# Moving key rotation, key zeros, sums of squares and an exponential table out of the first attention heads of a two-layer diffusion step

## Chip, cores and metric

One core of a Trainium2 chip (trn2) runs the whole program once. The metric is the device time of one execution in microseconds. Times below are device times or places in one profiled execution, counted from the start of its span.

## What is computed

The reference is one inference step of a two-layer backbone over 640 tokens (512 latent tokens of an 8 x 64 grid, 128 context tokens) with a model width of 1024. Each layer does:

```python
h = modulate(xs, norm_mix_g[l], sh_a, sc_a)            # RMSNorm, shift, scale
q_mla, c_kv, k_rope, na_q, na_k, na_v, gq, gk, gv = mixer_inputs(h, w_in[l], ...)
# MLA: c_q, c_kv are RMS-normed columns of z = h @ w_in; q_mla = c_q @ w_q_up; k_rope is rotated
# GQA: gq (6 heads) and gk (2 heads) are RMS-normed per head of 64, scaled, then rotated
o_na  = neighbourhood_attention(na_q, na_k, na_v, cache_na_k, cache_na_v, na_rpb)  # 4 heads
o_mla = blocked_attention(q_mla, [k_lat, k_ctx], [v_lat, v_ctx])                   # 6 heads
o_gqa = blocked_attention(rope(gq), [rope(gk), cache_gqa_k], [gv, cache_gqa_v])    # 6 heads
xs = xs + g_a * mix_out(o_mla, o_na, o_gqa, w_out[l])
xs = xs + g_f * swiglu(modulate(xs, ...), w_gate[l], w_up[l], w_down[l])
```

Context tokens attend only to context tokens. After the second layer comes one last RMSNorm. Keys and values of the context tokens are outputs too.

## The kernel before

Everything is fp32. A product with weights is three matmuls (`split_mm`, L631 to L633): both operands are split into a high part that ScalarE (ACT) rounds off and a low part that VectorE (DVE) gets by subtracting it (`lo`, L1323). So nearly every tile that TensorE (PE) reads has passed through ACT first and DVE second.

A layer has three stages. **Projection:** `z = h @ w_in` in 6 chunks of 304 columns, each chunk 5 tiles of 128 tokens. Tile number n = 5 * chunk + token tile goes to bank n % 6 of PSUM, ACT copies it to `z` (L1177), and PE starts tile n only when tile n - 6 has been copied. At the end of chunk 3 ACT sums squares of the MLA columns (L1192, L1194). In layer 0 DVE also has dot products for the modulation (`ada`, L1338), two per tile, some of them in each chunk. **Attention:** 16 heads, first 4 NA heads, then 6 MLA and 6 GQA heads. A head is 5 units: 4 blocks of 128 latent queries (i = 0 to 3) and the context block (i = 4). **Output projection and FFN.**

The order of work in the attention stage is one list, `SCHED`, made by `schedule()`. All engines walk through this same list, each doing its own part of every step. The list is cut in slots, one for each unit u = 5 * head + i: step `S` comes first in a slot, then what `extra` puts into it. Each engine executes strictly in order, so a step that waits holds up all that stands behind it on its engine. The steps that matter here:

- `S`: PE computes the scores (L846, L848 for NA heads), DVE adds the bias (L1562) and takes the maximum (L1568), ACT does the exponential of the unit before (L1132), DVE and POOL the reciprocal and the scaling (L495, L514) of the unit before that. PE needs the exponential of unit u - 2 for its bank.
- `M`: preparation of the next head's keys and queries: PE transposes (L702), ACT copies (L1081, L1069, L1078), DVE makes the low parts; `C`: cached keys (L1055, L1421, L1323). Steps `M` share bank 7, so each waits for the DVE part of the one before.
- `T`: transposition of the probabilities (L873, L1223, L1323), followed by the product with V.
- `CL`: DVE's low parts of the latents, two of 512 columns of `cqT` (L1460) and one of `ckvT`. `QU` n = 0 to 9: PE's product of `cqT` with `w_q_up` for one half of a token tile (6 matmuls of 288 columns), followed on ACT by the copy to `qm` (L1112). `CT`: the latents of the context tile, needed by QU 8 and 9. `QR` and `KR`: rotation of `qm` and of the MLA key by POOL (GpSimd; L1701, L1704, L1706). `BM`: POOL makes the bias of a head (L1765). `WK`: split of `w_kv_up`.
- `GS`, `GR` (layer 0 only): squares (ACT L1159) and sums (DVE L1485) of the GQA columns, one step for each token tile in slots 8 to 19, and the square root (L1163) in slot 21. In layer 1 the same squares and sums are done in the projection stage instead, at the end of chunk 3 on ACT and after the last split on DVE. `GZ`: scaling and rotation of the GQA columns (in layer 1 mostly before the heads).

The low parts of the keys have 64 rows of zeros for NA and GQA heads, set by DVE (L1421) when a head with new keys begins. `keep_busy` (L665) issues matmuls whose result is not used.

Of the kernel before, what the change touches and what calls it, by code (L numbers as in the profile page):

```python
# [19 lines left out]
F32 = mybir.dt.float32  # L20
# [5 lines left out]
P = 128  # L26
# [17 lines left out]
IC = 6  # L44
# [60 lines left out]
def schedule():  # L105
# [101 lines left out]
def build(nc, a, out):  # L207
    ctx = ExitStack()
    with ctx:
# [20 lines left out]
        warm = sb("warm", [P, 1])  # L230
# [142 lines left out]
        still_set = sem("still_set")  # L373
        win_first = sem("win_first")
# [254 lines left out]
        def _(pe):  # L629
# [132 lines left out]
            for l in range(DEPTH):  # L762
# [55 lines left out]
                for s in SCHED:  # L818
                    if s[0] == "S":
# [31 lines left out]
                        if u < 2:  # L851
                            keep_busy(4, 3)
                        if u == 9:
                            pe.wait_ge(qm_done, l * 2 * NT + 2 * NT)
                        if kind == "na" and u >= 9:
                            keep_busy(1, 2)
                    elif s[0] == "T":
# [19 lines left out]
                        def pv(g=g, mt=mt, n=n, a0=a0, a1=a1):  # L877
                            pair, slot = g // 2, g % 2
                            if slot == 0 and mt == 0:
# [133 lines left out]
        def _(sc):  # L1013
# [124 lines left out]
            for l in range(DEPTH):  # L1138
# [34 lines left out]
                for c in range(IC):  # L1173
                    for t in range(NT):
# [3 lines left out]
                        if c == 4 and t == (NT - 1 if (l == 0) else 1):  # L1178
# [9 lines left out]
                    if c == 3:  # L1188
# [20 lines left out]
                for s in SCHED:  # L1209
# [24 lines left out]
                    elif s[0] == "QU":  # L1234
# [11 lines left out]
                    elif s[0] == "GS" and l == 0:  # L1246
                        g_square(s[1], ztmp[:])
                    elif s[0] == "GR" and l == 0:
                        g_rms()
# [11 lines left out]
                sc.activation(warm[:], eps[:], ACT.Sqrt)  # L1261
                for o in range(KD):
# [6 lines left out]
                    if o == 2 and l + 1 < DEPTH:  # L1269
                        sc.wait_ge(cond_in, 32)  # L1270
                        sc.activation(silu_f[:], silu_f[:], ACT.Silu).then_inc(silu_done, 1)
                        sc.activation(warm[:], eps[:], ACT.Sqrt)
# [13 lines left out]
                sc.activation(warm[:], eps[:], ACT.Silu)  # L1286
# [23 lines left out]
                sc.activation(warm[:], eps[:], ACT.Sqrt)  # L1310
# [562 lines left out]
```

## Time and profile before

| | us |
|---|---|
| median of 3 runs | 1838.56 (1837.71 to 1839.36) |
| the profiled execution, own time | 1841.04 |
| its span in the profile | 1839.2 |
| PE busy | 1711.2 (93%) |
| DVE busy | 1164.6 (63%) |
| ACT busy | 692.7 (38%) |
| POOL busy | 215.3 (12%) |
| mean granted TensorE clock | 0.972 of full speed |

The profile follows one execution of the program. Its busy shares are averages over stages with different limits, so a stage has to be looked at by itself. Line numbers (L1568) are lines of the kernel; a tile is named without its buffer number. A number in brackets behind a row is the idle time of that engine just before the instruction, with the instruction that ended it.

### The profile page before, as it was taken

The numbers are of one execution on the slowest core, as the hardware profiler recorded it, in microseconds if no ns is written. First come the engines' busy times: TensorE is split into PE (matmuls) and PEld (weight loads), VectorE is DVE, ScalarE is ACT, GpSimd is POOL, SyncE is SP. The second block draws the span as 40 slices with busy tenths as digits, with TensorE's granted clock in tenths as the row PEclk, the third lists the DMA queues.
The fourth block names the chain that finished last, engine by engine and source line by source line (L and its number), as shares of the span: only waits on it lengthen the run. The fifth ranks groups of instructions, "written<-read, shape, count | busy, mean of one in ns | idle before, by whom it ended". The sixth has DMA issues, their size and how long they took to land.

```text
span 1839.2 us, 28458 instructions
## 1 busy us (share of the span) xinstructions
PE 1711.2 (93%) x11360; PEld 1657.6 (90%) x11360; DVE 1164.6 (63%) x2215; ACT 692.7 (38%) x1359; POOL 215.3 (12%) x316
## 2 busy tenths in 40 slices
PE   6899879889899999999989988988989999999997
PEld 6898777779899999999989977877989999999997
DVE  5996868848777777667552576786354544444443
ACT  2434756842422222222143376676342222222221
POOL 0003543310000000000010272332000000000001
PEclk9999999999899999999989989999989999999997
DMA  9461000053444433333132010002212222222201
GB/s 351 160 220 60 9 1 3 1 171 104 141 157 145 152 114 125 126 125 126 50 89 82 10 43 0 2 1 90 72 47 91 69 94 88 69 68 68 69 23 57
DMA packets 105525, 159.78 MB, mean 87 GB/s; under 512 B 5024, under 2 KB 83680, under 8 KB 105184
## 3 DMA queue, kind: packets, MB, share of 16 engines
q1 hardware_dynamic: 102800, 153.26, 24.8%
q10 hardware_dynamic: 2160, 3.23, 0.5%
q0 software_dynamic: 480, 2.19, 0.4%
q8 instruction: 49, 0.80, 0.2%
q14 instruction: 36, 0.29, 0.1%
HBM read 155.09 MB, written 3.57 MB: 86 GB/s over the span
## 4 chain that ended last, share of the span: by engine, by line
PE 82%; DVE 9%; ACT 3%; issue 2%; DMA 2%; POOL 1%; SPq 0%; POOLq 0%; DVEq 0%; ACTq 0%
PE ps L631 25%; PE ps L633 24%; PE ps L632 24%; PE ps L873 2%; PE ps L639 2%; DVE ps L1338 1%; DVE negmax L1568 1%; PE ps L846 1%; PE ps L848 1%; DMA ada_n<-in_w_ada_first 1%; DVE hT L1323 1%; DMA wo_raw<-in_w_out 1%; PE ps L702 1%; POOL rstd L1721 1%; DVE K L1323 1%
## 5 line engine op out<-in xcount | busy, mean ns | idle before, releaser
L631 PE MATMUL ps<-hT,gw 128*128 128x320 f32 x1408 | 437.6, 311 | 6.8 <-DVE hT L1323 6.8
L632 PE MATMUL ps<-hT,gw 128*128 128x320 f32 x1408 | 437.2, 311 | 0.0
L633 PE MATMUL ps<-hT,gw 128*128 128x320 f32 x1408 | 437.2, 310 | 0.0
L1402 DVE SCALAR_TENSOR_TENSOR x<-ps,mod,x 128x320 f32<-128x320 f32 (+2 forms) x576 | 211.6, 433 | 97.3 <-PE ps L633 94.3
L631 PEld LDWEIGHTS ps<-hT,gw 128*128 128x128 f32 x1408 | 265.8, 189 | 7.3 <-issue 7.3
L632 PEld LDWEIGHTS ps<-hT,gw 128*128 128x128 f32 x1408 | 265.8, 189 | 0.0
L633 PEld LDWEIGHTS ps<-hT,gw 128*128 128x128 f32 x1408 | 265.6, 189 | 0.0
L1654 DVE TENSOR_TENSOR mm<-sl,ps 128x320 f32<-128x320 f32 x88 | 42.7, 488 | 320.3 <-issue 185.3
L631 PE MATMUL ps<-act,dw 128*128 128x320 f32 x704 | 218.0, 310 | 2.7 <-DVE act L1323 2.7
L633 PE MATMUL ps<-act,dw 128*128 128x320 f32 x704 | 217.9, 309 | 0.0
L632 PE MATMUL ps<-act,dw 128*128 128x320 f32 x704 | 217.9, 309 | 0.0
L1293 ACT ACTIVATE sl<-ps 128x320 f32<-128x320 f32 x88 | 38.3, 438 | 445.6 <-PE ps L633 445.6
L631 PE MATMUL ps<-wi,hT 128*128 128x304 f32 x480 | 146.9, 306 | 12.1 <-DVE hT L1323 12.1
L633 PE MATMUL ps<-wi,hT 128*128 128x304 f32 x480 | 146.4, 305 | 0.0
L632 PE MATMUL ps<-wi,hT 128*128 128x304 f32 x480 | 145.8, 304 | 0.0
L631 PEld LDWEIGHTS ps<-act,dw 128*128 128x128 f32 x704 | 132.2, 188 | 2.9 <-DVE act L1323 2.9
L1300 ACT ACTIVATE act<-mm 128x320 fp32r<-128x320 f32 x88 | 41.3, 472 | 243.2 <-DVE mm L1654 243.2
L632 PEld LDWEIGHTS ps<-act,dw 128*128 128x128 f32 x704 | 132.2, 188 | 0.0
L633 PEld LDWEIGHTS ps<-act,dw 128*128 128x128 f32 x704 | 132.2, 188 | 0.0
L1718 POOL TENSOR_TENSOR rstd<-sq 128x640 f32<-128x640 f32 x2 | 3.1, 1566 | 1096.7 <-ACT sq L1022 1096.7
L1323 DVE TENSOR_TENSOR pT<-ps,pT 128x512 fp32r<-128x512 f32 (+2 forms) x176 | 109.1, 622 | 23.9 <-ACT pT L1223 22.4
L514 POOL TENSOR_SCALAR probs<-probs,rinv 128x640 f32<-128x640 f32 (+2 forms) x128 | 98.2, 768 | 180.5 <-DVE rinv L495 180.2
(212 smaller groups left out, 3574.7 us busy)
## 6 DMA issues: line engine op xcount, KB each, us to landing
ada_w<-in_w_adaT SPq DMA_DIRECT2D x48, 512.0 KB, 5.9
gw_raw<-in_w_gate SPq DMA_DIRECT2D x22, 1024.0 KB, 5.4
gw_raw<-in_w_up SPq DMA_DIRECT2D x22, 1024.0 KB, 8.0
dw_raw<-in_w_down SPq DMA_DIRECT2D x22, 1024.0 KB, 4.9
ada_wf<-in_w_adaT SPq DMA_DIRECT2D x34, 512.0 KB, 6.7
wi_raw<-in_w_in SPq DMA_DIRECT2D x12, 1216.0 KB, 6.7
wo_raw<-in_w_out SPq DMA_DIRECT2D x16, 512.0 KB, 5.1
ada_wq<-in_w_adaT SPq DMA_DIRECT2D x10, 512.0 KB, 4.8
```

The source lines that it names most:

```text
L514: po.tensor_scalar(t, t, rinv[:, u:u + 1], 1.0, ALU.mult, ALU.mult).then_inc(p_ready, 1)
L631: pe.matmul(dst, lh, rh, start=start, stop=False, skip_group_check=True)
L632: pe.matmul(dst, lh, rl, start=False, stop=False, skip_group_check=True)
L633: return pe.matmul(dst, ll, rh, start=False, stop=stop, skip_group_check=True)
L639: m = pe.matmul(ps[:, bank, 2 * t:2 * t + 2], tile[:, t * P:(t + 1) * P], ones[:, 0:2], start=first and t == 0, stop=last, skip_group_chec ...
L702: m = pe.transpose(ps[0:64, bank, o0:o0 + P], z[:, t, c0:c0 + 64], ident[:])
L873: m = pe.transpose(ps[:, 4 + n % 2, i * P:(i + 1) * P], probs[:, g % 2, i, pos:pos + P], ident[:])
L1293: sc.activation(sl[:, hf_], ps[:, 4 * j + hf_, 0:HALF], ACT.Silu).then_inc(sl_ready, 1)
L1300: sc.activation(act[:, j, 0, hf_ * HALF:(hf_ + 1) * HALF], mm[:, hf_], ACT.Copy).then_inc(act_hi, 1)
L1323: return ve.tensor_tensor(dst, src, f(hi), ALU.subtract)
L1402: i = ve.scalar_tensor_tensor(out=x[:, o, c0:c1], in0=ps[:, banks + hf_, s0:s0 + c1 - c0], scalar=mod[:, l, part * KD + o, q:q + 1], in1=x ...
L1654: ve.tensor_tensor(mm[:, hf_], sl[:, hf_], ps[:, 4 * j + 2 + hf_, 0:HALF], ALU.mult).then_inc(mm_ready, 1)
```

## The change

In `schedule()` the steps of the first slots are placed by hand. `CL` moves from slots 0 and 1 to slots 1 and 2. `QU` moves from the second half of slots 2 to 5 to slots 3 to 6, from slot 4 on ahead of the other extras; its copy on ACT becomes a step of its own (`QE`) at the slot's end. `CT` moves from slot 6 to the head of slot 7, `QU` 8 and 9 to the heads of slots 8 and 9. `KR`, `GS` and `GR` leave the list. PE's product waits for two `CL` steps and no longer for three; the first product with V waits for the third. DVE no longer clears key rows for NA heads, and does so only for GQA heads; POOL clears the low parts of all keys at once after the last split of `w_in`, and rotates the MLA keys after chunk 1. Layer 0 does squares, sums and root of the GQA columns where layer 1 does. After the root ACT executes one exponential on one column in both layers. `keep_busy(4, 3)` follows the first three units, before the first two.

```diff
-    spread([("CL", 0), ("CL", 1), ("CL", 2)], 0, 2)
-    for n in range(8):
-        extra[2 * (2 + n // 2) + 1].append(("QU", n))
-    extra[13].append(("CT", 3))
-    extra[15].append(("QU", 8))
-    extra[17].append(("QU", 9))
-    spread([("KR", t) for t in range(4)], 1, 4)
+    extra[3] += [("CL", 0), ("CL", 1)]
+    extra[5] += [("CL", 2)]
+    for n in range(0, 8, 2):
+        extra[6 + n] = [("QU", n), ("QU", n + 1)] + extra[6 + n]
+        extra[7 + n] += [("QE", n), ("QE", n + 1)]
+    extra[14] = [("CT", 3)] + extra[14]
+    for n in range(8, 10):
+        extra[2 * n] = [("QU", n)] + extra[2 * n]
+        extra[2 * n + 1].append(("QE", n))
     spread([("QR", t) for t in range(4)], 5, 8)
-    spread([("GS", t) for t in range(NT)] + [("GR",)], 8, 16)
...
-                pe.wait_ge(cT_ready, l * 4 + (3 if t < 4 else 4))
+                pe.wait_ge(cT_ready, l * 4 + (2 if t < 4 else 4))
...
-                        if u < 2:
+                        if u < 3:
                             keep_busy(4, 3)
-                        if u == 9:
+                        if u == 10:
                             pe.wait_ge(qm_done, l * 2 * NT + 2 * NT)
-                        if kind == "na" and u >= 9:
+                        if kind == "na" and u >= 10:
...
+                            if n == 0:
+                                pe.wait_ge(cT_ready, l * 4 + 3)
                             pe.wait_ge(pT_ready, l * TS + n + 1)
...
-                            if not (l == 0):
-                                g_rms()
+                            g_rms()
+                            sc.activation(warm[:, 3:4], eps[:], ACT.Exp)
...
-                        if l:
-                            sc.wait_ge(z_done, l * IC * NT + G_CHUNKS * NT)
-                            for t in range(NT):
-                                g_square(t, rstd[:, 0:512])
+                        sc.wait_ge(z_done, l * IC * NT + G_CHUNKS * NT)
+                        for t in range(NT):
+                            g_square(t, rstd[:, 0:512])
...
-                    elif s[0] == "QU":
+                    elif s[0] == "QE":
                         queries_out(l, s[1])
...
-                if kind == "gqa" or kind == "na" and h < 2:
+                if kind == "na" and h == 0:
+                    ve.wait_ge(key_zeros, l + 1)
+                if kind == "gqa":

                     ve.memset(K[64:P, kb, 1, :].bitcast(F32), 0.0)
...
-                        if l:
-                            for t in range(NT):
-                                g_sum(t, rstd[:, 0:512])
-                            g_mean()
+                        for t in range(NT):
+                            g_sum(t, rstd[:, 0:512])
+                        g_mean()
                     if l == 0:
                         for t in REST[REST_AT[c]:REST_AT[c + 1]]:
                             ada(l, t)
...
+                po.wait_ge(z_done, l * IC * NT + 2 * NT)
+                for t in range(4):
+                    if t:
+                        po.wait_ge(q_roped, l * 8 + t)
+                    rotate(l * OWN + 3 * t, 1, 32, z[:, t, OFF_KR:OFF_G].unsqueeze(1), rope[:, t, 0, 64:96], rope[:, t, 1, 64:96],
+                           rstd[:, LAT:LAT + 32].unsqueeze(1)).then_inc(q_roped, 1)
+                po.wait_ge(wi_ready, l * IC + IC)
+                settled(po, passed_po)
+                po.memset(K[:, :, 1, :].bitcast(F32), 0.0).then_inc(key_zeros, 1)
                 po.wait_ge(dots, 2 * dot_at(l, NADA - 1 if l else REST[-1]) + 2)
                 po.memset(still[:].bitcast(F32), 0.0).then_inc(still_set, 1)
```

## Rows read from the trace of the kernel before

**Rows 1.** The page: the chain that ended last, by engine.

```profile
PE 82%; DVE 9%; ACT 3%; issue 2%; DMA 2%; POOL 1%; SPq 0%; POOLq 0%; DVEq 0%; ACTq 0%
```

**Rows 2.** Both attention stages: stretch, length, busy us of PE, PEld, DVE, ACT, POOL, clock, DMA.

```profile
160.45:390.00 229.55, 196.83 (x1261) 171.26 (x1261) 178.19 (x403) 159.91 (x400) 97.84 (x149) 0.97 0.05 14
1058.75:1278.00 219.25, 194.92 (x1261) 171.41 (x1261) 169.57 (x386) 153.81 (x390) 86.81 (x138) 0.97 0.05 15
```

**Rows 3.** Timeline, DVE maxima: units 19, 21, 23 of layer 0, then 10, 19, 21, 23 of layer 1.

```profile
221.15 0.27 DVE L1568 TENSOR_REDUCE negmax<-ps 128x1 f32<-128x128 f32 x1
226.40 0.81 DVE L1568 TENSOR_REDUCE negmax<-ps 128x1 f32<-128x640 f32 x1
233.83 0.81 DVE L1568 TENSOR_REDUCE negmax<-ps 128x1 f32<-128x640 f32 x1
...
1093.33 0.56 DVE L1568 TENSOR_REDUCE negmax<-ps 128x1 f32<-128x384 f32 x1
1117.66 0.27 DVE L1568 TENSOR_REDUCE negmax<-ps 128x1 f32<-128x128 f32 x1
1124.96 0.82 DVE L1568 TENSOR_REDUCE negmax<-ps 128x1 f32<-128x640 f32 x1
1130.28 0.80 DVE L1568 TENSOR_REDUCE negmax<-ps 128x1 f32<-128x640 f32 x1
```

**Rows 4.** Stretch from unit 0 to unit 10 of layer 0.

```profile
165.69:195.32 29.63, 24.47 (x145) 22.21 (x144) 22.67 (x55) 20.71 (x59) 24.12 (x50) 0.83 0.13 38
```

**Rows 5.** Timeline, first slots of layer 0: PE's and DVE's waits around the products.

```profile
172.17 0.61 PE L631 MATMUL ps<-wq,cqT 128*128 128x288 f32 x1
...
175.22 0.41 PE L846 MATMUL ps<-K,Q 128*128 128x256 f32 x1
...
178.63 0.35 PE L631 MATMUL ps<-wq,cqT 128*128 128x288 f32 x1
...
180.28 0.28 PE L846 MATMUL ps<-K,Q 128*128 128x256 f32 x1
...
176.20 0.43 DVE L1562 TENSOR_TENSOR ps<-ps,bias_h 128x256 f32<-128x256 f32 x1 [2.21 <-PE ps L848]
...
180.89 0.43 DVE L1562 TENSOR_TENSOR ps<-ps,bias_h 128x256 f32<-128x256 f32 x1 [1.70 <-PE ps L848]
```

**Rows 6.** Timeline, ACT: table load of the first exponential; PE: what it releases.

```profile
167.47 1.28 ACT L1132 ACT_TABLE_LOAD   x1
...
169.49 0.45 PE L846 MATMUL ps<-K,Q 128*128 128x384 f32 x1 [0.58 <-ACT probs L1132]
```

**Rows 7.** Timeline, DVE: the zeros of head 1.

```profile
166.47 0.70 DVE L1421 MEMSET K<- 64x768 f32 x1 [0.22 <-issue]
```

**Rows 8.** Stretches at half clock, one in each layer.

```profile
171.00:177.60 6.60, 6.04 (x25) 5.61 (x26) 3.97 (x11) 3.68 (x13) 5.17 (x12) 0.50 0.16 48
1120.00:1123.40 3.40, 3.40 (x15) 3.30 (x16) 1.49 (x5) 0.80 (x2) 0.51 (x1) 0.51 0.00 0
```

**Rows 9.** Timeline, end of layer 0's projection: DVE, ACT; last, a sum in layer 1.

```profile
139.62 1.22 DVE L1338 SCALAR_TENSOR_TENSOR ps<-ada_wq,silu_c 128x1024 f32<-128x1024 f32 x1
...
150.25 0.21 DVE L1533 RECIPROCAL stat<-stat 128x10 f32<-128x10 f32 x1
...
160.98 0.70 DVE L1421 MEMSET K<- 64x768 f32 x1 [7.17 <-ACT K L1055]
...
146.64 0.42 ACT L1177 ACTIVATE z<-ps 128x304 f32<-128x304 f32 x1 [2.82 <-PE ps L633]
...
1034.27 0.69 DVE L1485 TENSOR_REDUCE stat<-rstd 128x8 f32<-128x512 f32 x1 [0.70 <-ACT rstd L1159]
```

**Rows 10.** DVE beside POOL: one scaling in layer 1; a POOL key rotation; chunks 2 to 5.

```profile
1048.48 1.78 DVE L1497 TENSOR_TENSOR z<-z,stat 128x512 f32<-128x512 f32 x1
...
176.49 0.25 POOL L1706 TENSOR_TENSOR z<-z,rstd 128x32 f32<-128x32 f32 x1
...
93.60:139.60 46.00, 46.00 (x332) 46.00 (x332) 44.38 (x62) 17.21 (x38) 0.00 (x0) 1.00 0.68 226
```

More of the change, by code:

```diff
@@ L229, in build @@
         eps = sb("eps", [P, 1])
-        warm = sb("warm", [P, 1])
+        warm = sb("warm", [P, 4])
         b_ada = sb("b_ada", [P, DEPTH, NADA])
@@ L373, in build @@
         still_set = sem("still_set")
+        key_zeros = sem("key_zeros")
         win_first = sem("win_first")
@@ L1177, in _ @@
                         sc.activation(z[:, t, c * ICW:(c + 1) * ICW], ps[:, n % 6, 0:ICW], ACT.Copy).then_inc(z_done, 1)
-                        if c == 4 and t == (NT - 1 if (l == 0) else 1):
+                        if c == 4 and t == (NT - 1 if l == 0 else 1):
                             sc.wait_ge(cstat_ms, 2 * l + 1)
                             sc.activation(stat[:, :, 0:2], stat[:, :, 0:2], ACT.Sqrt).then_inc(cstat_rms, 1)
-                            if not (l == 0):
-                                g_rms()
+                            g_rms()
+                            sc.activation(warm[:, 3:4], eps[:], ACT.Exp)
                     if c + 2 < IC:
@@ L1245, in _ @@
                         sc.activation(ckvT[:, 0, LAT:640], kc_mla[:], ACT.Copy).then_inc(wqk_hi, 1)
[L1246 to L1249, printed above, removed]
                     elif s[0] == "V":
@@ L1259, in _ @@
                         i.then_inc(v_hi, 1)
-                sc.activation(warm[:], eps[:], ACT.Sqrt)
+                sc.activation(warm[:, 0:1], eps[:], ACT.Sqrt)
                 for o in range(KD):
@@ L1271, in _ @@
                         sc.activation(silu_f[:], silu_f[:], ACT.Silu).then_inc(silu_done, 1)
-                        sc.activation(warm[:], eps[:], ACT.Sqrt)
+                        sc.activation(warm[:, 0:1], eps[:], ACT.Sqrt)
                 def gw_split(b, j):
@@ L1285, in _ @@
                 modulated(l, 1)
-                sc.activation(warm[:], eps[:], ACT.Silu)
+                sc.activation(warm[:, 0:1], eps[:], ACT.Silu)
                 def ffn_block(b, last):
@@ L1309, in _ @@
                 ffn_block(FB - 1, True)
-                sc.activation(warm[:], eps[:], ACT.Sqrt)
+                sc.activation(warm[:, 0:1], eps[:], ACT.Sqrt)
                 sc.wait_ge(act_ready, (l + 1) * FB * 4 + 1)
@@ L1594, in _ @@
                         lo(ckvT[:, 1, LAT:640], kc_mla[:], ckvT[:, 0, LAT:640]).then_inc(wkv_ready, 1)
-                    elif s[0] == "GS" and l == 0:
-                        g_sum(s[1], ztmp[:])
-                    elif s[0] == "GR" and l == 0:
-                        g_mean()
                     elif s[0] == "V":
@@ L1729, in g_rotate @@
                         po.wait_ge(g_roped, l * 4 + t)
-                    rotate(l * OWN + (24 if l == 0 or t >= LATE_G else 0) + 3 * t, 8, 64, view, rope[:, t, 0, 0:64], rope[:, t, 1, 0:64], tmp).then_inc(g_roped, 1)
+                    rotate(l * OWN + (24 if l == 0 or t >= LATE_G else 12) + 3 * t, 8, 64, view, rope[:, t, 0, 0:64], rope[:, t, 1, 0:64], tmp).then_inc(g_roped, 1)
                     po.wait_ge(g_roped, l * 4 + t + 1)
@@ L1746, in _ @@
                 value_zeros(0)
-                turned = 0
                 for s in SCHED:
@@ L1770, in _ @@
                             window(po, l, h + 1)
-                    elif s[0] in ("KR", "QR"):
+                    elif s[0] == "QR":
                         t = s[1]
-                        if s[0] == "QR":
-                            po.wait_ge(qm_done, l * 2 * NT + 2 * t + 2)
-                        if turned:
-                            po.wait_ge(q_roped, l * 8 + turned)
-                        if s[0] == "KR":
-                            n, view = 1, z[:, t, OFF_KR:OFF_G].unsqueeze(1)
-                        else:
-                            n, view = 6, qm[:, t, :].rearrange("p (h d) -> p h d", h=6)[:, :, 64:96]
-                        tmp = rstd[:, 0:32 * n].rearrange("p (h d) -> p h d", h=n)
-                        rotate(l * OWN + (3 * LATE_G if l else 0) + 3 * turned, n, 32, view, rope[:, t, 0, 64:96], rope[:, t, 1, 64:96],
+                        po.wait_ge(qm_done, l * 2 * NT + 2 * t + 2)
+                        po.wait_ge(q_roped, l * 8 + 4 + t)
+                        view = qm[:, t, :].rearrange("p (h d) -> p h d", h=6)[:, :, 64:96]
+                        tmp = rstd[:, 0:192].rearrange("p (h d) -> p h d", h=6)
+                        rotate(l * OWN + 12 + (3 * LATE_G if l else 0) + 3 * t, 6, 32, view, rope[:, t, 0, 64:96], rope[:, t, 1, 64:96],
                                tmp).then_inc(q_roped, 1)
-                        turned += 1
                     elif s[0] == "S":
```

## The prediction, made before the changed kernel was run

> **What bounds the kernel now.** I read the chain of waits first: 82% of it is PE, 9% DVE [rows 1], so a change away from PE pays only where PE waits. Then the busy time by stretch. The attention stages are the loose places: layer 0 spends 229.6 us there with PE busy 196.8, layer 1 219.3 us with PE busy 194.9, for the same matmuls [rows 2]. The two layers run one schedule, so I put the maxima of DVE side by side, unit by unit, which is the view that prices this change. From unit 10 (195.32, where the stretch of rows 4 ends) to unit 19, layer 0 takes 25.83 us and layer 1 24.33 [rows 3, 4]: the squares and sums cost 1.50 us there. From unit 21 to 23 layer 0 takes 7.43 and layer 1 5.32 [rows 3]: 2.11 us for the square root, which switches ACT's table away from the exponential and back. The first 10 units take 29.63 us, of which DVE is busy 22.67 [rows 4], so 7 us of its time are waits. The large ones are for PE: 2.21 and 1.70 us [rows 5], each for scores queued behind two query products. That queueing is what the new order addresses. The end of an attention stage releases the next weights and PE's output projection, so I pass each microsecond saved there on to the end.
>
> **Squares, sums, root (layer 0).** Removed from the heads: 1.50 + 2.11 = 3.6 us. One of the five squares lies before unit 10, and I take 0.2 for it, since DVE was waiting there anyway: 3.8 us, between 3.4 and 4.1.
>
> **Their new place.** ACT does square 0 at once, but for square 1 it waits for DVE's first sum, and that stands behind the last weight split, which ends just before the dots at 139.62 [rows 9]. Behind ACT's wait stand its copies of `z`. In layer 1 one round of square and sum takes 0.69 + 0.70 = 1.39 us [rows 9]. So the sums end about 4 x 1.39 + 0.7 = 6.3 us later, at 145.9, the last square at about 145.1, and the first held copy (tile 20) at 145.5. PE needs it for tile 26, which it starts when tile 25 ends, at 146.64 [rows 9]: 1.1 us of slack. DVE's dots, 139.62 to 150.25, end at 156.5, and what follows them is late by the same 6.3 us; before, DVE then stood idle for 7.17 us until 160.98 [rows 9]. It fits, narrowly. The root adds nothing there, as ACT is waiting for PE. The sum has 0.3 us of loss for this item, the range 0 to 2.9 (below).
>
> **POOL's new work before the heads.** Four key rotations of four short instructions, 0.25 us or less each [rows 10], after chunk 1, and one clearing of the keys after the last split. Nothing else is queued on POOL: its next item waits for the dots. But DVE is busy 44.38 of the 46.00 us of that stretch [rows 10], so what it loses there moves the first sum. One DVE instruction of layer 1 took 1.78 us beside POOL [rows 10], where the sum of equal size took 0.69. If each of 16 rotations delays DVE by its own 0.25, that is 4.0 us, less 1.1 slack = 2.9; if none does, 0. I take about 1.4, since the short ones mostly fall into gaps between dots: 0.3 after the slack. The Trainium skill ("SBUF — State Buffer", "SBUF: two separate sides") has the rule that speaks against this part: a DVE instruction with two SBUF inputs and a GpSimd instruction that reads SBUF exclude each other for a whole instruction. By it the loss would be at the 2.9 end.
>
> **The exponential's table.** The first exponential waits for 1.28 us of table load in each layer, and PE's third unit stood 0.58 us for it [rows 6]. Early, the load meets an idle ACT. Alone it is worth 0.6 (PE's wait) to 1.28 us a layer; it is inside the next sum. The Trainium skill ("ScalarE: Activation LUTs", "What ACT_TABLE_LOAD costs") gives 2.66 us for a switch, with a drain of 1.38. By it the heads would gain up to 1.4 more a layer. The trace shows 1.28 alone: the root's two loads cost 2.11 together.
>
> **Zeros and key rotation.** Head 0's clearing lay under ACT's key copies: worth 0. Head 1's 0.70 us [rows 7] counts only as DVE work removed. POOL's scaling was not what PE waited for, so the rotation's place is worth 0 by itself; what covers it is POOL's lead of some microseconds in slots 5 to 8.
>
> **The query products.** In the new list the scores of unit 3 go before products 0 and 1, so DVE's 2.21 us wait goes, and the scores of unit 5 stand behind products 2 and 3 alone, which go out while DVE splits V: the 1.70 us goes too. With the 0.70 of clearing that is 4.6 us a layer. What is late next: products 4 and 5 now stand ahead of the key transposes of head 2 in PE's queue, two products that take 1.65 us at full clock (178.63 to 180.28) and 3.05 at half (172.17 to 175.22) [rows 5]. ACT's copies and DVE's low part of head 2's keys start that much later against unit 5, and products 6 and 7 wait for ACT, whose `qm` copies stand behind those key copies. A pair of products at full clock is 1.65 us, a little of it covered by DVE's own work, so I take back 1.3: **3.3 us a layer.** Ends: 4.6 if later slack swallows it, 1.3 if only the table counts. The extra `keep_busy` (3 matmuls) stands where PE waits for the exponential and the next queries: 0.
>
> **Sum.** 2 x 3.3 + 3.8 - 0.3 = 10.1 us. The profiled execution's 1841.04 gives 1830.9; the median of the runs is 2.5 us lower, so against it I predict **1828.5**. 0.2%, some 3.7 us, is about what a measurement of this kernel can tell from no change.
>
> **Rivals.**
> *The clock goes with the waits (20%).* Products 0 to 3 ran at a granted clock of 0.50 [rows 8], the lower of its levels (1.2 GHz), after PE had idled three times while it waited for head 1's low parts and the exponential. If PE still idles enough before them, or in the new wait for ACT's copies, 4 of the 8 products run at half: 1.4 us for each pair. Then, or if the table is not kept to the first exponential (1.3 a layer), the heads give 1.5 a layer: 3.0 + 3.8 - 0.3 = 6.5, 1832.0. For: both layers show this stretch. Against: PE has three more matmuls and scores ahead of the first product.
> *The first heads give it back (8%).* If DVE or POOL is the bound of units 5 to 15, whatever PE gains is waited away, and only layer 0's 3.5 remains: 1835.1, no change that can be told. For: DVE is busy 22.67 and POOL 24.12 of 29.63 us [rows 4]. Against: differences between the layers stay from one unit to the next once they arise, and POOL loses four rotations of about 1.1 us there.
> *More than that (8%).* The clock fell in layer 1 at 1120 and not in layer 0: units 19 to 21 took 7.30 against 5.25 [rows 3, 8]. Without it, and with 4.6 a layer, the gain is 9.2 + 3.8 + 2.05 = 15: 1823.5.
> *Slower (2%).* Place: ACT's queue in layer 0's projection, where one late sum holds all copies of `z` and through them PE's tile 26. It decides once the first sum is late by 1.1 + 10.1 us. Behind the dots (10.6 us), delayed by POOL (4.0), and each sum lengthened as in rows 10 (5 x 1.1 = 5.5), that is 20.1 - 1.1 = 19.0 us of stall, less 10.4: 1847. Against: in the code the sums stand ahead of the dots.
>
> **How the numbers follow.** The forecast has 62%, with a range of its own from 1825.5 (4.6 a layer) to 1832 (2.9 lost, 2.8 a layer). The first rival lies at its upper end; to take in the clock's share at both ends and part of the larger gain the range is 1824.0 to 1833.5, leaving out the 8% near 1835, the slower case and about half of the larger one. Faster by over 0.2% (below 1834.9): 62 + 20 + 8 = 90%; same 8%; slower 2%.
>
> **What would show it.** Right: unit 10 of each layer 2.8 to 4 us nearer to unit 0; layer 0 like layer 1 from unit 10 to 23 but for clock stretches; a table load at L1183 or so beside an idle ACT; no root among the heads; attention stages of about 222 and 216 us. A step is wrong if PE shows idleness before tile 26 (squares' place), if DVE's dots grow beyond 1.23 us after chunk 1 (POOL), if a pair of products takes 3 us (clock), or if DVE waits over 1.3 us for head 2's keys (order). The forecast is wrong if layer 0's projection grows by more than 3 us, or if unit 20 lies no earlier than before.

## Result, and the profile after

| | before | after |
|---|---|---|
| median of 6 runs each, same chip, us | 1838.25 (1835.68 to 1839.36) | **1828.37** (1825.34 to 1832.24) |
| ratio to before, 95% interval | | 0.995 (0.9939 to 0.996) |
| the profiled execution, own time / span | 1841.04 / 1839.2 | 1825.34 / 1823.5 |
| its mean granted clock | 0.972 | 0.981 |

The gain of the medians is 9.9 us; 10.1 were predicted. The two profiled executions differ by 15.7, because the one of before is among its slowest and the one of after is the fastest of its six. So the traces say where time went, and the medians how much. Of the 15.7 us, 11.9 lie between the first and the last unit of the two layers' heads and 0.3 ahead of them. The other 3.5 lie in the stages between and behind the heads, where half-clock stretches fell differently.

The page after: the busy line, the granted clock in 40 slices and the chain that ended last, by engine.

```profile
PE 1697.8 (93%) x11362; PEld 1644.9 (90%) x11362; DVE 1162.3 (64%) x2211; ACT 689.9 (38%) x1359; POOL 233.1 (13%) x318
PEclk9999999999999999999979999999989999999998
PE 77%; DVE 13%; ACT 4%; issue 3%; DMA 2%; POOL 1%; SPq 0%; POOLq 0%; DVEq 0%; ACTq 0%
```

POOL is busy 18 us longer although it has two instructions more; why is below. Stretches of after, columns as in [rows 2]: both attention stages, the first ten units of both layers [rows 4], and chunks 2 to 5 of the projection [rows 10].

```profile
160.45:383.00 222.55, 192.44 (x1262) 167.45 (x1262) 173.87 (x395) 152.89 (x390) 94.44 (x133) 0.99 0.05 14
1050.00:1264.30 214.30, 190.02 (x1262) 166.47 (x1262) 168.20 (x384) 152.06 (x389) 82.36 (x122) 1.00 0.05 15
165.38:191.75 26.37, 20.91 (x146) 18.59 (x144) 21.83 (x53) 18.63 (x58) 20.08 (x31) 1.00 0.14 43
1055.39:1081.15 25.76, 20.52 (x143) 18.28 (x142) 22.04 (x53) 18.71 (x57) 19.11 (x31) 1.00 0.14 43
93.60:139.60 46.00, 46.00 (x333) 46.00 (x332) 44.38 (x60) 16.31 (x35) 16.07 (x16) 1.00 0.68 226
```

The attention stages lost 7.0 and 5.0 us. The ten units lost 3.26 in layer 0 and 3.67 in layer 1, and their clock is full where it was 0.83 in layer 0. DVE's maxima of units 10, 19, 21 and 23 of layer 0 [rows 3]:

```profile
191.75 0.56 DVE L1568 TENSOR_REDUCE negmax<-ps 128x1 f32<-128x384 f32 x1
...
216.11 0.27 DVE L1568 TENSOR_REDUCE negmax<-ps 128x1 f32<-128x128 f32 x1
...
221.96 0.81 DVE L1568 TENSOR_REDUCE negmax<-ps 128x1 f32<-128x640 f32 x1
...
227.14 0.81 DVE L1568 TENSOR_REDUCE negmax<-ps 128x1 f32<-128x640 f32 x1
```

Unit 10 to 19 takes 24.36 us (25.83 before), 19 to 21 5.85 (5.25), 21 to 23 5.18 (7.43): 3.1 us in all. For the experiments I measure each unit's maximum from that of unit 0. Unit 14 is there because the first ten units turned out not to hold the whole effect. Each * stands for 3.4 us at half clock before that mark. That is 1.7 us of full-speed time, but the mark moves by less where PE has waits that take it up.

| us after unit 0 | L0: 6 | 10 | 14 | 19 | L1: 6 | 10 | 14 | 19 |
|---|---|---|---|---|---|---|---|---|
| before | 18.35** | 29.63*** | 41.08*** | 55.46*** | 18.17** | 29.43*** | 39.96*** | 53.76*** |
| before_busy3 | 16.36 | 26.97 | 38.56 | 52.94 | 16.32 | 26.83 | 38.45 | 52.24 |
| order_only | 16.63 | 28.75* | 40.25* | 54.64* | 16.58 | 27.29 | 38.45 | 52.23 |
| old_order | 16.20 | 27.35* | 37.89* | 51.68* | 16.12 | 26.26 | 36.79 | 50.58 |
| kr_back | 16.28 | 26.58 | 38.66 | 52.46 | 16.25 | 28.32* | 38.90* | 52.69* |
| wait3 | 18.56* | 28.59* | 39.16* | 52.96* | 18.72* | 28.74* | 39.32* | 53.11* |
| after | 16.36 | 26.37 | 36.95 | 50.73 | 16.01 | 25.76 | 36.34 | 50.12 |
| after_again | 16.29 | 26.30 | 36.89 | 50.68 | 16.24 | 26.04 | 36.63 | 50.42 |
| keys_first | 14.84 | 24.81 | 35.39 | 49.17 | 14.88 | 26.85* | 37.38* | 51.18* |

The first slots of layer 0 after, timeline, as in [rows 5, 6]: PE's waits at the query products, then DVE's, then ACT's first exponential.

```profile
171.58 0.40 PE L633 MATMUL ps<-wq,cqT 128*128 128x288 f32 x1 [0.56 <-DVE cqT L1461]
...
174.98 0.37 PE L633 MATMUL ps<-wq,cqT 128*128 128x288 f32 x1 [0.96 <-ACT qm L1116]
...
181.09 0.37 PE L633 MATMUL ps<-wq,cqT 128*128 128x288 f32 x1 [1.28 <-ACT qm L1116]
...
177.25 0.43 DVE L1562 TENSOR_TENSOR ps<-ps,bias_h 128x256 f32<-128x256 f32 x1 [0.25 <-PE ps L850]
...
180.54 0.68 DVE L1322 TENSOR_TENSOR K<-ps,K 64x512 fp32r<-64x512 f32 x1 [2.02 <-ACT K L1085]
...
167.31 0.58 ACT L1136 ACTIVATE probs<-ps,negmax 128x384 f32<-128x384 f32 x1
```

The waits of 2.21 and 1.70 us are gone, and the exponential starts without a load. DVE now waits 2.02 us for head 2's keys, and PE 1.28 for ACT's copies of products 4 and 5.

### The profile page after: what moved, and what is told of

Its sections match the earlier page's. It is cut to its first block, busy times and chain, and to the rows that moved or that the text cites. A ratio compares the mean times of both kernels' runs of the same rounds, so it can differ in the third digit from the quotient of the medians.

```text
span 1823.5 us, 28464 instructions
## 1 busy us (share of the span) xinstructions
PE 1697.8 (93%) x11362; PEld 1644.9 (90%) x11362; DVE 1162.3 (64%) x2211; ACT 689.9 (38%) x1359; POOL 233.1 (13%) x318
## 4 chain that ended last, share of the span: by engine, by line
PE 77%; DVE 13%; ACT 4%; issue 3%; DMA 2%; POOL 1%; SPq 0%; POOLq 0%; DVEq 0%; ACTq 0%
PE ps L633 23%; PE ps L635 22%; PE ps L634 22%; DVE ps L1337 5%; PE ps L875 2%; PE ps L641 2%; DVE negmax L1568 1%; PE ps L848 1%; DVE hT L1322 1%; PE ps L704 1%; DMA ada_n<-in_w_ada_first 1%; PE ps L850 1%; DMA wo_raw<-in_w_out 1%; DVE K L1322 1%; POOL rstd L1717 1%
```

## Experiments

The kernels ran in three jobs. Before's median was 1838.17 (26 runs), 1837.31 (17) and 1838.28 (18). Ratios are to before of the same job, with a 95% interval. They are not quotients of the medians (old_order: ratio 0.9977, medians 0.9986), and the two measures can differ by up to 1.7 us, so where only one of them shows a difference I say so.

**First job: single parts.** `order_only` is before with the new order and what came with it (steps, waits and the third `keep_busy`):

```
-    spread([("CL", 0), ("CL", 1), ("CL", 2)], 0, 2)
...
+    extra[3] += [("CL", 0), ("CL", 1)]
...
-                        if u < 2:
+                        if u < 3:
                             keep_busy(4, 3)
```

> The kernel before with the new places of CL, QU, QE and CT alone (with the shorter wait and the third keep_busy); table, zeros, key rotation, squares and root stay where they were. Theory A (order): the gain of the first heads is that of the queue of PE. Unit 10 of both layers comes 2 to 2.5 us nearer to unit 0 than before (29.63 and 29.43 us), since the 1.28 us of table load still stand before the first exponential; units 10 to 23 of layer 0 as before, 38.5 us. Rival B (table): the load and the zeros carry it; then unit 10 gains under 1 us. Rival C (clock): what counts is that no stretch at half clock falls on the products; if one falls there again, unit 10 gains under 1.5 us though the order is new. Median 4 to 5 us below before under A.

`before_busy3` is before with nothing but `if u < 3:` there.

> The kernel before with three more unused matmuls behind the scores of unit 2 and nothing else. Theory A (order): PE's idleness before the products stays, DVE's waits for scores behind products stay; unit 10 within 0.5 us of before (29.63 and 29.43 us) and the stretch at half clock from unit 2 on stays. Rival C (clock): the stretch at half clock goes, and units 0 to 10 shorten by 1.5 us or more in both layers; then that much of the gain of the changed kernel belongs to its clock.

`squares_back` is the change with layer 0's squares, sums and root back in slots 8 to 16 (`spread([("GS", t) ...] + [("GR",)], 8, 16)`, and `if l:` before the early ones).

> The changed kernel with the squares, sums and root of layer 0 back among its heads. Theory A (as in the sum, corrected by the two traces): unit 10 of layer 0 hardly later (0.2 us), units 10 to 30 of layer 0 longer by 3.1 us than in the changed kernel (58.1 us), of which the root makes 2.1 to 2.3 between units 21 and 23; DVE's idleness of 7 us before the first keys of layer 0 is back, and PE's first transposes start 0.2 us earlier. Rival: the sums in the projection stage cost PE something that units do not show, so that taking them back costs less than 2.5 us in all. Layer 1 unchanged. Median 3 us above the changed kernel.

`no_table` is the change without the one-column exponential:

```
                             g_rms()
-                            sc.activation(warm[:, 3:4], eps[:], ACT.Exp)
```

> The changed kernel without the early exponential; the 1.28 us of load are back before the first exponential in both layers. Theory A: the load is on the path of the scores of unit 2 and through DVE's maximum of unit 2 on all that follows, so unit 10 of both layers comes 0.8 to 1.3 us later than in the changed kernel (26.37 and 25.76 us). Rival: DVE's two cqT parts, which now stand between the maxima of units 1 and 2, cover it as they did before; then unit 10 moves by less than 0.3 us. By the page of the Trainium skill on activation tables (a switch costs 2.66 us) it would be 2.2 us or more. Median 1.5 to 2.5 us above the changed kernel under A.

Measured: order_only 1835.38 us (10 runs), 0.9992 (0.9979 to 1.0006), which can't be told from before; before_busy3 1834.18 (10), 0.998 (0.9968 to 0.9992); squares_back 1831.38 (9), 0.9966 (0.9956 to 0.9977); no_table 1830.74 (6), 0.9967 (0.9954 to 0.9979).

The order was to bring 3.3 us a layer. order_only, which has the third `keep_busy` too, lies 2.8 us below before by the medians and 1.5 by the ratio, whose interval includes no change. before_busy3, with three unused matmuls more in each layer and nothing else, which were to bring nothing, lies 4 us below. The intervals of the two overlap; in layer 1, where both keep the clock, unit 14 lies at the same 38.45. So the order adds nothing that shows to the third `keep_busy` here. The timeline of before_busy3, DVE's waits at units 3 and 5 [rows 5], then PE's:

```profile
175.13 0.43 DVE L1562 TENSOR_TENSOR ps<-ps,bias_h 128x256 f32<-128x256 f32 x1 [0.49 <-PE ps L848]
...
179.52 0.43 DVE L1562 TENSOR_TENSOR ps<-ps,bias_h 128x256 f32<-128x256 f32 x1 [0.87 <-PE ps L848]
...
197.50 0.44 PE L873 MATMUL ps<-ident,probs 128*128 128x128 f32 x2 [1.07 <-POOL probs L514]
```

In before's own order the 2.21 and 1.70 us shrink to 0.49 and 0.87, with the clock at 1.00. So most of these waits came from the products running at half clock, not from their place in the queue. What is late next is POOL: PE stands 1.07 us for its scaling of the probabilities, and 1.29 us at 183.34. In order_only the longest such wait is 0.58 us, in layer 1. The table of units says it in time: before_busy3 gains 2.60 us by unit 10 of layer 1, and only 1.51 are left at unit 14.

squares_back, DVE's maxima of units 21 and 23 of layer 0, and ACT between them:

```profile
222.48 0.81 DVE L1576 TENSOR_REDUCE negmax<-ps 128x1 f32<-128x640 f32 x1
...
229.91 0.81 DVE L1576 TENSOR_REDUCE negmax<-ps 128x1 f32<-128x640 f32 x1
...
223.64 1.28 ACT L1168 ACT_TABLE_LOAD   x1
...
225.46 1.28 ACT L1137 ACT_TABLE_LOAD   x1
```

7.43 us, as before the change, against 5.18: the root costs 2.25 with its two loads of 1.28. From unit 10 to 21 the squares cost 31.11 - 30.21 = 0.90, together 3.15 us, and the median is 3.0 above the change's.

no_table: ACT's load stands ahead of the exponential again, and PE waits for it, as in [rows 6]:

```profile
167.64 1.28 ACT L1136 ACT_TABLE_LOAD   x1
...
169.66 0.44 PE L848 MATMUL ps<-K,Q 128*128 128x384 f32 x1 [0.58 <-ACT probs L1136]
```

Yet unit 10 lies at 26.33 and 26.25 us, against 26.37 and 25.76 of the change's first trace and 26.30 and 26.04 of after_again. Behind the 0.58 us PE had to wait for the first query latents anyway (0.56 above, 0.48 here). The medians (1830.74 against 1828.4) differ by 2.4, but the intervals of the two ratios overlap. By the marks the table is worth nothing in layer 0 and 0.2 to 0.5 us in layer 1; more is not shown.

**Second job: interactions.** `after_again` is the change unaltered; `old_order` is the change with before's order but three `keep_busy`; `busy2` the change with `if u < 2:`.

> The changed kernel once more, unchanged, on the chip of its three companions: the base of their comparison, and the clock of more executions. All theories: median 1828 to 1830 us. If the clock of an execution sets its place in the spread, time falls as the mean granted clock rises, by about 1.2 us for each 0.001, and its head stages differ from the first trace only by stretches at half clock.

> The changed kernel with the old places of CL, QU and CT and the old waits; table, zeros, key rotation, squares, root and the third keep_busy as in the change. Theory C (clock and the small parts; the order is worth nothing): unit 10 at 25.3 to 25.9 us, from 26.83 us of the kernel before with the third keep_busy, less 0.5 for the table and up to 1.0 for zeros and rotation; median equal to the changed kernel within 1.5 us. Theory A of the prediction (the order is worth 3.3 us a layer): unit 10 at 28 us or later in both layers, even with the clock full, and the median 4 us or more above the changed kernel.

> The changed kernel with keep_busy behind the first two units only, as before. Theory C: the three unused matmuls behind unit 2 are what keeps the clock; without them a stretch at half clock falls on products 0 to 3 again, unit 10 moves by 1 to 2.5 us in both layers, the mean granted clock falls by 0.003 or more, the median rises by 3 us or more. Theory A: scores of unit 3 before the products and the early table keep PE busy enough; clock and units stay within 0.3 us, and the median within 1.5 us.

`keys_first` puts head 2's keys ahead of products 4 and 5, which the 2.02 us wait suggests:

```
     for n in range(0, 8, 2):
-        extra[6 + n] = [("QU", n), ("QU", n + 1)] + extra[6 + n]
+        if n == 4:
+            extra[10] += [("QU", 4), ("QU", 5)]
+        else:
+            extra[6 + n] = [("QU", n), ("QU", n + 1)] + extra[6 + n]
```

> The changed kernel with products 4 and 5 behind the key transposes of head 2 instead of ahead of them. The wait of DVE for those keys (2.02 us in the changed kernel) shrinks by the 1.65 us of two products. Theory A: unit 6 comes 1 to 1.6 us earlier, and unit 10 in both layers 0.5 to 1.5 us earlier (26.37 and 25.76 us), the median 1 to 3 us lower. Rival: the products are as late as ACT's copies let them be, the rest of the chain (qm copies, CT, products 8 and 9) keeps its times, and unit 10 moves by less than 0.3 us.

Measured: after_again 1827.8 us (5), 0.9952 (0.9939 to 0.9965); old_order 1834.68 (12), 0.9977 (0.9963 to 0.9991); busy2 1827.63 (6), 0.9945 (0.993 to 0.996); **keys_first 1824.96** (6), 0.9935 (0.9916 to 0.9954).

Among the change's other parts the third `keep_busy` is worth nothing (busy2), in before 4 us (before_busy3). The new order does not keep the clock without it. busy2's trace has a stretch at half clock in both layers, half as long as that of before [rows 8]; layer 0:

```profile
170.00:173.50 3.50, 3.36 (x14) 3.17 (x15) 3.39 (x8) 1.53 (x6) 2.15 (x3) 0.52 0.04 15
```

But it costs nothing: unit 10 lies at 26.39 and 26.13 us, unit 14 at 36.98 and 36.71, as in the change. The waits that the change has at its first products (0.56 and 0.96 us above) take it up: in layer 0 of busy2 they add up to 0.45, in layer 1 to 0.56. So the clock fell as theory C said, and the marks stayed as theory A said.

At full clock in both, old_order and the change differ little: layer 1's unit 14 at 36.79 against 36.34 and 36.63. But old_order's median is 6.9 us above (4.6 by the ratios, whose intervals just touch). Its mean granted clock over 12 runs is 0.9754, the change's over 5 is 0.9786, and within old_order the time follows the clock: 1825.69 us at 0.981, 1838.63 at 0.972. Its trace has one such stretch in layer 0's first ten units (186 to 191) that the change's traces don't have:

```profile
186.00:191.00 5.00, 4.59 (x25) 4.54 (x26) 4.34 (x11) 2.29 (x8) 4.67 (x11) 0.66 0.24 75
```

In front of it PE waited 2.05 us before products 8 and 9, for the last tile of `ckvT`:

```profile
186.41 0.43 PE L630 MATMUL ps<-wq,cqT 128*128 128x288 f32 x1 [2.05 <-DVE ckvT L1317]
```

The change moves `CT` 3, which makes that tile, and its wait there is 1.09 and 0.85 us. Over the 14 profiled executions of this study, two layers each, this wait was 1.81 to 2.16 us nine times, and six times a half-clock stretch stood behind it; it was 0.84 to 1.39 us nineteen times, and never did one. The place alone does not set this wait: before_busy3 has the old place and waits 1.27 and 1.28 us, order_only has the new one and waits 1.81 and 1.82. With the rotation moved, the new order has the shorter wait.

That is a small part of the 6.9 us. The profiled executions of old_order and after_again differ by 8.0 us, and only 1.0 and 0.2 of it lie before unit 14 of the two layers. Another 2.7 lie in the rest of the heads, and 5.7 between the last unit of layer 0 and the first of layer 1, where both kernels run the same code (old_order, then after_again):

```profile
375.82:1062.54 686.72, 659.83 (x4438) 654.39 (x4437) 441.98 (x779) 201.27 (x312) 34.78 (x42) 0.97 0.34 115
372.63:1053.64 681.01, 655.74 (x4436) 650.25 (x4435) 441.70 (x778) 201.26 (x312) 34.77 (x42) 0.98 0.34 116
```

In the 14 profiled executions this stretch takes 681.0 to 687.9 us. Whether old_order's clock is lower there because of its order or by chance is open, so the order's worth over the whole run is not shown beyond the marks.

keys_first in its trace: the wait of 2.02 is 0.39.

```profile
179.07 0.68 DVE L1325 TENSOR_TENSOR K<-ps,K 64x512 fp32r<-64x512 f32 x1 [0.39 <-ACT K L1088]
```

Unit 6 comes 1.5 us earlier in layer 0 (14.84) and 1.1 to 1.4 in layer 1 (14.88); in layer 1 PE waited 1.87 us before products 8 and 9, and a half-clock stretch behind it took the gain back by unit 10.

**Third job: what was costed at nothing, and the shorter wait.** `kr_back` puts the change's key rotation back between the heads; `dve_zeros` puts the clearing for heads 0 and 1 back on DVE and drops POOL's; `wait3` keeps the new order but waits for three compressed tiles; `keys_first_busy` adds fillings to keys_first.

```
+    spread([("KR", t) for t in range(4)], 1, 4)
...
```

> The change, with its key rotation put back among the first heads (four steps of GpSimd between the queries' rotations, from unit 1 on); nothing else differs. Theory A, the prediction's (worth 0: each step takes GpSimd some 0.25 us and GpSimd has slack): the median stays within 1 us of the change, 1827 to 1829 us, and layer 0's ten units stay at 26.3 us. Theory B (once the waits for the keys are short, TensorE waits for GpSimd's scaling of the queries and its probabilities instead, as the kernel before with three fillings showed with waits of 1.29 and 1.07 us <-POOL): TensorE's waits that end by POOL appear in the first ten units, together 0.3 to 1.0 us, unit 10 comes at 26.6 to 27.3 us, and the median rises by twice that, 0.6 to 2 us, or by more if the granted clock falls there: each fall of it in these units has cost 1.7 us.

```
-                if kind == "gqa":
+                if kind == "gqa" or kind == "na" and h < 2:
...
```

> The change, with the clearing of the second half of the key tile for heads 0 and 1 back on VectorE (0.70 us each where it ran in the kernel before, two per layer). The prediction put its removal at 0. If right: the median within 1 us of the change, unit 10 within 0.1 us of 26.3 us, VectorE's 1.40 us coming out of waits that it has (2.02 us for the keys' scaling). If VectorE bounds the first heads, unit 10 comes later by up to 0.70 to 1.40 us in each layer, and the median by 1.4 to 2.8 us.

```
-                pe.wait_ge(cT_ready, l * 4 + (2 if t < 4 else 4))
+                pe.wait_ge(cT_ready, l * 4 + (3 if t < 4 else 4))
```

> The change, with the queries' product in its new place but waiting for three of the compressed keys' tiles where the change waits for two. Theory A (the shorter wait is what lets the product stand in its new place): the first products of queries start near 174.0 us in place of 171.6 us, everything behind them in TensorE's queue moves with them, unit 6 comes 0.5 to 2 us later than at 16.4 us and unit 10 at 27 to 28 us, and the clock may fall again behind the longer idle stretch; the median rises by 1 to 5 us. Theory B (the third tile is there in time, and only the order counts): no wait of TensorE for it above 0.1 us, unit 10 at 26.3 us, the median within 1 us of the change.

```
-                        if u < 3:
-                            keep_busy(4, 3)
+                        if u < 5:
+                            keep_busy(4, (3, 3, 3, 2, 4)[u])
```

> The change, with the second head's query products behind its keys' (the version that measured 1824.96 us, 0.9935 of the kernel before), and two and four unused products behind units 3 and 4, where TensorE waited 0.56 and 0.96 us. Theory A (what those waits cost is the granted clock, which fell in layer 1's first ten units in that version's trace): no half-clock stretch before unit 10 in either layer, ten units in 24.8 us in both, mean granted clock 0.980 or more, median 1822 to 1825 us. Theory B (the clock there is as it was and the fillings only take TensorE's time, or stand in front of products that wait): unit 10 at 25.0 to 25.5 us and a median of 1825 to 1828 us. It also shows again whether the version with the keys first is below the change, which gave 1827.8 and 1828.4 us.

Measured: **kr_back 1833.31 us** (7), 0.9965 (0.9953 to 0.9978); dve_zeros 1828.12 (5), 0.9946 (0.9929 to 0.9963); wait3 1830.8 (10), 0.996 (0.9948 to 0.9972); keys_first_busy 1825.49 (6), 0.9933 (0.9919 to 0.9946).

kr_back's median is about 5 us above the change. Its ratio is 2.4 to 3.5 us above those of the change and dve_zeros, with intervals that overlap, so it is the marks that show the loss. Either is more than theory B's upper end without a fall of the clock, and I had looked for it at the wrong place: unit 10 of layer 0 is 0.2 late, unit 14 is 1.7 late at full clock. In layer 1 unit 14 is 2.3 to 2.6 late; there PE waited 1.95 us before products 8 and 9, and half clock followed. POOL's timeline in layer 0, one of four rotation steps with the scaling behind it, and two later scalings, then PE:

```profile
177.33 0.39 POOL L1698 TENSOR_TENSOR rstd<-z,rope 128x16 f32<-128x16 f32 x2
177.79 0.25 POOL L1701 TENSOR_TENSOR z<-z,rope 128x32 f32<-128x32 f32 x1
178.13 0.25 POOL L1703 TENSOR_TENSOR z<-z,rstd 128x32 f32<-128x32 f32 x1
178.35 0.81 POOL L517 TENSOR_SCALAR probs<-probs,rinv 128x512 f32<-128x512 f32 x1
...
191.99 1.50 POOL L517 TENSOR_SCALAR probs<-probs,rinv 128x512 f32<-128x512 f32 x2
...
196.82 0.44 PE L876 MATMUL ps<-ident,probs 128*128 128x128 f32 x2 [1.52 <-POOL probs L517]
```

A step takes 178.35 - 177.33 = 1.0 us, four of them 4. The same 30 us of kr_back and of the change:

```profile
175.00:205.00 30.00, 24.84 (x174) 22.35 (x175) 23.70 (x64) 21.26 (x66) 27.05 (x56) 1.00 0.09 26
```

```profile
175.00:205.00 30.00, 26.29 (x184) 23.78 (x185) 25.28 (x68) 22.99 (x69) 24.57 (x41) 1.00 0.09 26
```

POOL is busy 27.05 against 24.57 us, PE does ten matmuls fewer, and the clock is full in both. POOL's queue holds no wait above 0.3 us in kr_back from 175.4 to 203, so those 4 us arrive some slots later at the scalings for which PE transposes. The rotation's place is worth 1.7 us a layer at full clock, which before_busy3 against old_order gives too (layer 1's unit 14: 38.45 - 36.79), and more where it lengthens a wait that costs clock. It fits that order_only, with the rotation still among the heads, is no better than before_busy3. By which path it is held there is not shown: PE waits for POOL 0.58 us at most, and 1.8 before products 8 and 9.

dve_zeros changed nothing: DVE's 2.02 us wait stood there unchanged. wait3, PE's timeline, the first product:

```profile
175.12 0.40 PE L633 MATMUL ps<-wq,cqT 128*128 128x288 f32 x1 [3.03 <-DVE ckvT L1322]
```

In the new place the third tile comes late: 3.03 us of wait, the product 2.2 us later against unit 0 (2.4 expected), half clock behind it (granted 0.57 from 176 to 180), unit 14 2.2 us later in layer 0 and 2.7 to 3.0 in layer 1. Its profiled execution is among its slowest (1835.96); the median is 2.7 us above dve_zeros, the intervals overlap, and four of its ten runs (1827.6 to 1828.5) are as fast as the change. So in the trace the shorter wait is worth 2.2 to 3.0 us a layer in the new place; over the runs it is less clear.

keys_first_busy kept the clock in both layers' first ten units:

```profile
166.37:192.16 25.79, 22.24 (x151) 19.38 (x150) 23.04 (x53) 18.72 (x57) 18.61 (x31) 1.00 0.15 44
1054.66:1079.39 24.73, 22.05 (x151) 19.28 (x150) 21.64 (x52) 18.57 (x57) 19.06 (x31) 1.00 0.16 45
```

Layer 1 is 1.0 us better than the change, layer 0 0.6. In layer 0 the six more matmuls end the 0.96 us wait, but the one before products 8 and 9 grows from 1.25 to 1.85 us. In the median they are worth nothing against keys_first. keys_first lies 2.8 us below the change of its job, keys_first_busy 2.6 below dve_zeros, which equals the change. The intervals overlap, so "2 to 3 us" is the best estimate rather than a shown difference.

## Why the prediction was right, and where it was not

**The total** (10.1 predicted, 9.9 measured) was right, but its largest term was right by luck. The 3.3 us a layer were costed as the products' place in the queue; the marks find them mostly in two things that the text had at nothing, the clock under the third `keep_busy` and the place of the key rotation. The sources, against the steps:

- *Squares, sums, root: 3.8 us, right in kind, oversized.* Measured 3.15 by the trace of squares_back and 3.0 by the median. The root was 2.25 (2.11 in the text). The squares were 0.9, not 1.5 + 0.2: DVE's maximum of unit 19 stood behind the last sum, a delay that unit 21 no longer had. A mark taken just behind an added instruction counts its whole length.
- *Their new place: 0.3 us, right, and its working held to 0.3 us.* The end of layer 0's projection after (compare [rows 9]): DVE's second and last sum, ACT's last square, its first held copies, the early table load, DVE's end of the dots, PE's first transposes.

```profile
141.19 0.69 DVE L1486 TENSOR_REDUCE stat<-rstd 128x8 f32<-128x512 f32 x1 [0.70 <-ACT rstd L1163]
...
145.34 0.69 DVE L1486 TENSOR_REDUCE stat<-rstd 128x8 f32<-128x512 f32 x1 [0.70 <-ACT rstd L1163]
...
144.67 0.63 ACT L1163 ACTIVATE rstd<-z 128x512 f32<-128x512 f32 x1 [0.75 <-DVE stat L1486]
145.21 1.66 ACT L1181 ACTIVATE z<-ps 128x304 f32<-128x304 f32 x5
...
147.11 1.28 ACT L1186 ACT_TABLE_LOAD   x1
...
156.78 0.21 DVE L1533 RECIPROCAL stat<-stat 128x10 f32<-128x10 f32 x1
```

  The last square starts at 144.67 and ends at 145.3 (145.1 predicted), the copies start at once, 1.4 us ahead of 146.64, and the dots end at 156.8 (156.5). PE has no wait there. One was not named: PE's first transposes of the next stage come behind `mod`, which follows the dots. It costs about 0.2 us.

- *POOL beside DVE: 1.4 us of delay for DVE. Wrong side.* DVE's busy time from 93.6 to 139.6 is 44.38 us before and after, and its last split starts 0.18 us later (137.06 against 136.88). POOL paid:

```profile
94.65 1.11 POOL L1700 TENSOR_TENSOR z<-z,rope 128x32 f32<-128x32 f32 x1
...
104.02 2.58 POOL L1702 TENSOR_TENSOR z<-z,rstd 128x32 f32<-128x32 f32 x1
```

  The instruction of 0.25 us [rows 10] takes 1.1 to 2.6 us here. The page of the Trainium skill cited in the prediction ("SBUF — State Buffer", "SBUF: two separate sides") has the two exclude each other for a whole instruction; that fits these lengths. That it would put the loss at the 2.9 end is not borne out: beside a DVE that was hardly ever idle it was POOL that waited, and POOL had nothing else to do until 139.9. This is also where most of POOL's 18 us of added busy time comes from.

- *The table: 0.6 to 1.28 us a layer, within the order's sum.* The load left the path (147.11 above, 1.28 us), but it is worth 0 to 0.5 us a layer, since PE's next wait hid most of its 0.58. The 2.66 us for a switch of the Trainium skill ("ScalarE: Activation LUTs", "What ACT_TABLE_LOAD costs") was not seen: each load in these traces is 1.28 us and the next activation follows within 0.02.
- *Zeros: 0, right* (dve_zeros). *Key rotation: 0, wrong: 1.7 us a layer at full clock (2.4 to 5 us in kr_back's runs, by ratio or by median).* The text said "POOL's scaling was not what PE waited for". That was true of a trace in which PE was late by half clock. The cover was POOL's lead, and this same change uses it up. I had the cover named, and the fall of it costed nowhere.
- *The query products' order: 3.3 us a layer.* The size was right for layer 1 (3.3 to 3.6 at unit 14 for all parts together), the cause not. At the marks of layer 1, where unit 14 stands for what lasts: the clock alone 1.5 (before to before_busy3), the rotation and the table 1.7 (to old_order), the order 0.2 to 0.5 (to the change). The shares hold for this sequence of steps: in busy2 the new order makes the half clock cost nothing without the third `keep_busy`, and no run has the old order with two `keep_busy` among the other parts of the change, which would tell what the order is worth then. The take-back of 1.3 was also low: DVE waits 2.02 us for head 2's keys, beyond the 1.3 that the text set as the mark of a wrong step. What the order has besides, with the rotation moved, is the shorter wait before products 8 and 9; in old_order a half-clock stretch stood behind the longer one in layer 0, 1.0 us at unit 14.
- *`keep_busy`: 0.* Right for the change (busy2), where PE's waits take up the half clock, but the same three matmuls bring 4 us in before.

**The rivals.** "The clock goes with the waits" had the right resource and the wrong sign of independence: the clock was not a remainder behind the waits but the cause of most of them (2.21 and 1.70 us became 0.49 and 0.87), and it did recover. "More than that" needed the fall at 1120 in layer 1 to go, which it did in the profiled execution (15.7 us between the traces) but not in after_again, where units 19 to 21 of layer 1 take 7.30 us again; the medians do not show it. Its price of 2.05 us was too high: without the fall these units take 5.85 us, so it costs 1.45. The 5.25 of layer 0 before, which the text compared with, had unit 19 late behind the sums. "The first heads give it back" is near to what kr_back does by unit 14 through POOL; the change has the rotation out of the way.

**The sum in the experiments' terms**, from the marks: 3.1 (squares and root) - 0.2 (new place) + 2 x 3.3 to 3.6 (layer 1's unit 14) = 9.5 to 10.1 us. By the medians the runs that undo one part add up to more (squares 3.0, rotation 5, order 6.9), which would fit parts that share one clock and one queue. By the ratios they add up to 10 to 11 (2.6 to 2.9, 2.4 to 3.5, 4.6), so this is not shown.

## What to carry to other kernels

A wait behind matmuls that ran at half clock is not yet a fault of the order: before costing a reorder, work out the wait again with those matmuls at full clock, or run the kernel with a few unused matmuls more. Where a step is costed at zero because an engine has a lead, subtract from that lead what the other parts of the same change gain; the lead of POOL was gone at half of the gain. Measure a moved step some slots behind its place, since a queue without waits delivers its delay later (unit 14 here, not unit 10). And before giving a difference of two traces to an edit, see in which stage it lies: here a stretch of some 685 us that the edits hardly touch differed by up to 6.9 us.

## What was not expected of the hardware

- How much of the result is clock: before lost three pieces of 1.7 us to half clock in the first heads of each layer, the change none, and the mean granted clock over the runs rose from 0.9744 (17 of before) to 0.9786 (5 of the change), which is 0.0042 x 1838 = 7.7 us of full-speed time. But the mean clock does not give the time: before_busy3's is 0.9792 over 10 runs, no lower than the change's, and it is 4 us faster than before, not 10. Runs of one kernel differ by such pieces: old_order spans 12.9 us between 0.981 and 0.972.
- One wait of PE, the one before products 8 and 9, stood in front of six of the twelve half-clock stretches in the first ten units of all traces: nine waits of 1.81 to 2.16 us with six stretches behind them, nineteen of 0.84 to 1.39 with none. (The other six are in before, busy2 and wait3, around the first products.) It is no rule by itself: layer 1 of old_order waited 2.05 us and kept its clock, as did keys_first_busy after 1.85 and layer 1 of order_only after 1.82. What else decides remains open.
- A stretch at half clock can cost nothing: busy2's 3.4 us in each layer left unit 14 within 0.4 us of the change, as PE had waits behind it.
- POOL instructions of 32 columns that take 0.25 us among the heads took 1.1 to 2.6 beside DVE's dots and splits, with no loss for DVE beyond 0.2 us in 46.
